# A convolution stage's end: where the modulation units run, and an output product as three rounded passes

## The chip, the cores and the metric

One core of a Trainium2 chip runs the whole program: three blocks of a network with modulated (adaptive) norms in float32, one launch. Engines are named as in the profile: PE (TensorE, matmul), PEld (its weight loads), DVE (VectorE), ACT (ScalarE), POOL (GpSimd) and SP (SyncE, which issues the DMAs). The metric is the device time of one execution in microseconds (us). The kernel before took 4165.31 us (median of 3 runs, 4162.82 to 4167.35).

## The reference, cut to what matters

The change lies in the convolution mixer of the first block. `h` is the normalized and modulated input (512 tokens of 1024 channels), and E is 2048:

```
a, g, z   = split(h @ conv_w_in + conv_b_in, 3)      # (512 x 1024) @ (1024 x 6144)
v         = a * sigmoid(g)
v         = depthwise_conv2d_rowwise(v, conv_dw, 31 taps, rows of 64) + conv_dw_b
v         = layernorm over E of v, times conv_ln_g, plus conv_ln_b
v         = silu(v) * silu(z)
x         = x + gate * (v @ conv_w_out + conv_b_out)  # (512 x 2048) @ (2048 x 1024)
```

The modulation vectors of blocks two and three are computed in the same stage, beside this, since they depend on nothing but their condition vectors:

```
mod2 = silu(c_2) @ w_ada_2 + b_ada_2                  # (1 x 1024) @ (1024 x 6144)
mod3 = silu(c_3) @ w_ada_3 + b_ada_3
```

All inputs are float32.

## The kernel before, in words

The program is a row of phases, each a block in which every engine has its own instruction list and semaphores order them; a phase begins when the one before it has ended on all engines. Activations lie transposed: channels on the 128 partitions, 512 tokens along a row. `conv_phase` (L978) is the phase in question. It runs in the trace from 1217.0 to 1821.1 us.

**Products.** 48 products in an order fixed by `by_tile` (L993): for tile i of 16, the SIG product (sigmoid gate), the A product (value), and the GATE product (outer gate) of tile i-2. Each is 8 float32 matmuls of 128x128 weights and 512 columns (L1113) into one of 6 PSUM banks used in a ring. PE's float32 matmul appears as two MATMUL records in the trace. `wait_bank` (L1029) makes PE wait until the bank's last reader is done. ACT evicts SIG (L1165) and GATE (L1168); DVE evicts A with the sigmoid into a padded grid (`padded`, L1208, instruction L1211).

**Taps.** DVE applies the 31 taps of two tiles at a time, alternating between them (L1225, L1228): 62 instructions for a pair, into `u`. PE adds up finished tiles with a matmul of ones (`total`, L1081, L1083) for the mean, five tiles behind the products.

**Modulation units.** The two 1024x6144 matrices are cut into `NA` = 48 units of 256 columns, 1 MB each, loaded by SP into two buffers `cv_ada` (`load_ada`, L1043; a load waits for the unit two before it to have been multiplied). One unit (`modulation`, L1092) is 8 matmuls of 32-column weights (L1102), in four row groups of the array's output, followed by `turn` of the unit before it (L1085, L1088, two narrow matmuls), which adds and transposes the four partial sums. ACT's `taken` (L1149) copies the unit's sums out (L1153) and then keeps the turned unit before it (`keep`, L1145, L1147). A unit's first matmul waits until ACT has copied the sums of the unit before and kept the one before that.

Where a unit runs is decided by `spread` and `unit_at` (L1003, L1004): `spread` units lie among the products, after product `FIRST + ...`, and all others follow in a loop behind the last product (L1120).

**The stage's end.** Behind the last unit PE turns it (L1123), adds the last totals (L1125), and DVE forms the mean (L1235) and subtracts it from 16 tiles (L1238). ACT adds the bias to `xT` (L1177), squares each tile (L1182, four buffers), and PE adds the squares (L1129) for the variance. ACT makes 1/sqrt with Ln and Exp (L1185, L1187). Then, tile by tile, DVE multiplies by it (L1241, L1244), ACT applies gain, bias and silu (L1190), DVE multiplies by the outer gate (L1246), and PE multiplies the tile with the 8 column blocks of `conv_w_out` into all 8 banks (L1137): 16 tiles x 8 float32 matmuls. DVE adds the banks to `xT` (L1254).

SP's queue is in program order: product weights and unit loads interleaved (L1067 to L1073), the loads of the remaining units (L1074), the last output weights (L1076).

A float32r tile holds float32 rounded to fewer mantissa bits; a matmul of two such tiles makes one pass. Other phases of this kernel already split both operands in a rounded part and a rest and add three passes: high x high, high x rest, rest x high (for example L594 to L596, L3309 to L3311).

## Time and profile before

| what | value |
|---|---|
| median of 3 runs | 4165.31 us |
| profiled execution, its own time | 4166.43 us |
| its span | 4164.7 us |
| mean granted clock of PE over the span | 0.945 |
| PE busy / DVE busy / ACT busy / POOL busy | 91% / 46% / 31% / 14% |

The span is the time from the first to the last instruction of the one profiled execution. The granted clock is 1.00 at 2.4 GHz and 0.50 at 1.2 GHz. In a row of the timeline the first number is the start of a run of like instructions, the second how long it lasts, `x16` their number, and in brackets the idle time of the engine before it and what ended it. Matmuls overlap, so a row's length is longer than the distance to the next start. In rows of groups the columns are line, engine, operation, tiles and shapes, count | busy us, mean ns of one | idle time before, and what ended it.

### The profile page before, as it was taken

Reading aid. Unit: us, or ns where it says so; the run is one execution under the profiler, and the core shown is the slowest. Engines: PE = TensorE matmul, PEld = TensorE weight load, DVE = VectorE, ACT = ScalarE, POOL = GpSimd, SP = SyncE. Lnnn points to the kernel's source line nnn. Section 1 sums busy time; section 2 is a strip of 40 time slices with the busy share of each in tenths; the row PEclk is TensorE's granted clock in tenths of the full one; section 3 lists DMA queues with packets and bytes.
Section 4 is the critical chain, followed back from the end, with each engine's and each line's share of the span. In section 5 each row is a group of like instructions: output and inputs, shape, how many; then the busy total and the mean of one; then the engine's idle time right before and its main releaser. Section 6 shows DMA issues by size and latency. Waiting matters only on the chain. (4 is left out here: it accounts for less than half of the span.)

```text
span 4164.7 us, 58511 instructions
## 1 busy us (share of the span) xinstructions
PE 3807.4 (91%) x24493; PEld 2707.3 (65%) x24493; DVE 1927.8 (46%) x3055; ACT 1290.4 (31%) x2231; POOL 580.3 (14%) x303
## 2 busy tenths in 40 slices
PE   5899999999689998989999999999898858999998
PEld 2688888888554444445455555788675847777876
DVE  1455565555419886243213323543267656245421
ACT  0544444444321121332113322432343031323321
POOL 0000000000110000010000001344361000443442
PEclk7899999999799997899889999999999979999999
DMA  8211111111235456120402113233230000432331
GB/s 298 61 42 46 52 52 37 42 52 51 61 106 168 152 156 199 49 77 27 91 8 62 45 31 101 86 97 97 62 88 18 4 1 3 114 94 84 93 92 60
DMA packets 515096, 318.67 MB, mean 77 GB/s; under 512 B 30908, under 2 KB 497397, under 8 KB 514582
## 3 DMA queue, kind: packets, MB, share of 16 engines
q1 hardware_dynamic: 514838, 314.87, 26.0%
q8 instruction: 206, 3.38, 0.3%
q14 instruction: 52, 0.43, 0.0%
HBM read 310.64 MB, written 4.19 MB: 76 GB/s over the span
## 5 line engine op out<-in xcount | busy, mean ns | idle before, releaser
L1113 PE MATMUL cv_bank<-hT,cv_w 128*128 128x512 f32 x768 | 340.2, 598 | 13.8 <-DMA cv_w<-in_conv_w_in_dram 13.8
L3274 POOL TENSOR_TENSOR tl_wl<-tl_w,tl_wh 128x1024 fp32r<-128x1024 f32 (+1 forms) x104 | 246.8, 2374 | 718.8 <-ACT tl_wh L3385 718.7
L1228 DVE SCALAR_TENSOR_TENSOR conv_u<-cv_pad,vec,conv_u 128x512 f32<-128x512 f32 x480 | 319.2, 741 | 0.0
L1113 PEld LDWEIGHTS cv_bank<-hT,cv_w 128*128 128x128 f32 x768 | 144.9, 191 | 188.2 <-issue 173.6
L2164 POOL TENSOR_TENSOR mp_wl<-mp_w,mp_wh 128x1024 fp32r<-128x1024 f32 x72 | 173.3, 2409 | 597.0 <-ACT mp_wh L2244 597.0
L3385 ACT ACTIVATE tl_wh<-tl_w 128x1024 fp32r<-128x1024 f32 (+1 forms) x104 | 108.5, 1043 | 356.8 <-PE tl_bank L3311 354.6
L594 PE MATMUL hg_bank<-hg_hh,hg_wh 128*128 128x512 f32 x512 | 208.5, 407 | 0.0
L596 PE MATMUL hg_bank<-hg_hh,hg_wl 128*128 128x512 f32 x512 | 200.3, 391 | 0.0
L595 PE MATMUL hg_bank<-hg_hl,hg_wh 128*128 128x512 f32 x512 | 199.0, 389 | 0.0
L3309 PE MATMUL tl_bank<-tl_room,tl_wh 128*128 128x512 f32 x464 | 186.8, 403 | 12.9 <-POOL tl_wl L3274 12.1
L3311 PE MATMUL tl_bank<-tl_room,tl_wl 128*128 128x512 f32 x464 | 183.2, 395 | 0.0
L3310 PE MATMUL tl_bank<-tl_room,tl_wh 128*128 128x512 f32 x464 | 181.8, 392 | 0.0
L1952 PE MATMUL at_bank<-hT,at_w 128*128 128x512 f32 x384 | 177.6, 606 | 0.0
L912 POOL TENSOR_TENSOR ho_wl<-ho_w,ho_wh 128x2048 fp32r<-128x2048 f32 x7 | 33.1, 4730 | 1015.2 <-ACT ho_wh L941 1015.2
L583 PE MATMUL hg_bank<-hg_w,hT 128*128 128x128 f32 x1024 | 133.2, 294 | 35.2 <-issue 19.3
L583 PEld LDWEIGHTS hg_bank<-hg_w,hT 128*128 128x128 f32 x1024 | 131.2, 210 | 43.5 <-issue 27.1
L2244 ACT ACTIVATE mp_wh<-mp_w 128x1024 fp32r<-128x1024 f32 x72 | 76.1, 1059 | 251.5 <-PE mp_bank L2184 244.0
L3309 PE MATMUL tl_bank<-tl_hh,tl_wh 128*128 128x512 f32 x352 | 139.4, 396 | 4.3 <-DVE tl_rest L3489 4.3
L3311 PE MATMUL tl_bank<-tl_hh,tl_wl 128*128 128x512 f32 x352 | 139.4, 396 | 0.0
L3310 PE MATMUL tl_bank<-tl_rest,tl_wh 128*128 128x512 f32 x352 | 139.3, 396 | 0.0
L2182 PE MATMUL mp_bank<-mp_dh,mp_wh 128*128 128x512 f32 x320 | 129.0, 403 | 0.0
L771 DVE TENSOR_TENSOR hg_wl<-hg_w,hg_wh 128x1024 fp32r<-128x1024 f32 x64 | 78.1, 1221 | 103.5 <-ACT hg_wh L678 103.5
(693 smaller groups left out, 8199.6 us busy)
## 6 DMA issues: line engine op xcount, KB each, us to landing
cv_ada<-in_w_ada_dram SPq DMA_DIRECT2D x48, 1024.0 KB, 7.8
hg_w<-in_hgrn_w_in_dram SPq DMA_DIRECT2D x80, 512.0 KB, 3.9
mp_w<-in_w_mlp_dram SPq DMA_DIRECT2D x64, 512.0 KB, 4.0
ada_w<-in_ada_w_dram SPq DMA_DIRECT2D x12, 2048.0 KB, 19.9
cv_w<-in_conv_w_in_dram SPq DMA_DIRECT2D x48, 512.0 KB, 4.0
tl_w<-in_w_ffn_in_dram SPq DMA_DIRECT2D x44, 512.0 KB, 3.9
fr_w<-in_w_in_dram SPq DMA_DIRECT2D x26, 512.0 KB, 3.8
at_w<-in_w_in_dram SPq DMA_DIRECT2D x24, 512.0 KB, 3.9
```

What stands on the lines that cost most here:

```text
L583: ins = pe.matmul(bank[:, t * P:(t + 1) * P], src[:, k, t * P:(t + 1) * P], W[m][:, k, :], start=(k == 0), stop=(k == KD - 1))
L594: pe.matmul(bank[:, :], wh[:, k, :], hh[:, k, :], start=(k == 0), stop=False)
L595: pe.matmul(bank[:, :], wh[:, k, :], hl[:, k, :], start=False, stop=False)
L596: ins = pe.matmul(bank[:, :], wl[:, k, :], hh[:, k, :], start=False, stop=(k == KD - 1))
L1113: ins = pe.matmul(ps[n % RING][:, :], W[n % SLOTS][:, k * P:(k + 1) * P], K.hT[:, k, :], start=(k == 0), stop=(k == KD - 1))
L1228: ins = dve.scalar_tensor_tensor(o, x, by, o, ALU.mult, ALU.add)
L1952: ins = pe.matmul(SIDE_BANK[:, :], W[n % WS][:, k, :], K.hT[:, k, :], start=(k == 0), stop=(k == KD - 1))
L2164: pool.tensor_tensor(WL[u % SPLIT][:, :, :], W[(UPS + u) % RAW][:, :, :], WH[u % SPLIT][:, :, :].bitcast(F32), ALU.subtract).then_inc(low, 1)
L3274: pool.tensor_tensor(WL[u % SPLIT][:, 0:n, :], W[u % RAW][:, 0:n, :], WH[u % SPLIT][:, 0:n, :].bitcast(F32), ALU.subtract).then_inc(low, 1)
L3309: pe.matmul(to[:, :], wh[:, wk, :], rh[:, k, :], start=first, stop=False)
L3310: pe.matmul(to[:, :], wh[:, wk, :], rl[:, k, :], start=False, stop=False)
L3311: ins = pe.matmul(to[:, :], wl[:, wk, :], rh[:, k, :], start=False, stop=last)
```

## The change

The units: `spread` becomes 38 (31 before), so 38 units lie among the products, placed by `FIRST + a * 44 // 38`. Six follow the last product. The last four (44 to 47) are put between the matmuls of the variance, behind those of tiles 4, 7, 10 and 13; ACT's `taken` of each comes after its next square, and the last turn and keep come after the variance.

The output product: `conv_w_out` and the gated tiles are split in a rounded part and a rest. ACT makes the rounded parts (`WH` of 1024 columns, `uH` of 512), DVE the rests (`WL`, `uL`), and PE makes three passes for each of the 128 matmuls. `uL` takes the place of `u` and `uH` that of `gate` in memory, `WL` that of the padded grids and `WH` that of the sigmoids. The weights' split has two buffers each; the first two are converted by ACT between the last keep and the Ln. The whole diff:

```diff
--- before.py
+++ after.py
@@ -975,7 +975,7 @@
 CW, CP, GW = 31, 15, 64
 
 
-def conv_phase(K, u, gate):
+def conv_phase(K, u, gate, uL, uH):
 
 
     nc, inp = K.nc, K.inp
@@ -999,12 +999,17 @@
     ada = [inp[name][0].rearrange("(k p) n -> p k n", p=P) for name in ("w_ada_2", "w_ada_3")]
     AC, AW = 256, 2
     NA = 2 * 6 * DM // AC
-    FIRST, OF4 = 4, 3
-    spread = OF4 * (3 * NT_ - BEHIND - FIRST) // 4
-    unit_at = {FIRST + 4 * a // OF4: a for a in range(spread)}
+    FIRST, MIXED = 4, 10
+    spread = NA - MIXED
+    unit_at = {FIRST + a * (3 * NT_ - FIRST) // spread: a for a in range(spread)}
+    beside = {4 + 3 * n: spread + 6 + n for n in range(MIXED - 6)}
     with ExitStack() as st:
         W = [K.sb(st, f"cv_w{s}", [P, KD * P]) for s in range(SLOTS)]
+        with ExitStack() as under:
+            WL = [K.sb(under, f"cv_wl{s}", [P, KD * P], F32R) for s in range(2)]
         pad = [K.sb(st, f"cv_pad{p}", [P, rows, GW + 2 * CP]) for p in range(4)]
+        with ExitStack() as under:
+            WH = [K.sb(under, f"cv_wh{s}", [P, KD * P], F32R) for s in range(2)]
         sig = K.sb(st, "cv_sig", [P, 4, T])
         mean = K.sb(st, "cv_mean", [P, T])
         rstd = K.sb(st, "cv_rstd", [P, T])
@@ -1023,6 +1028,7 @@
          bg_ok, xb_ok, out_p, out_d) = sems[SLOTS:SLOTS + 19]
         extra = K.more_sems()
         (ada_in0, ada_in1, ada_sum, ada_turn, ada_copied, ada_kept, cond_ok) = extra[:7]
+        w_high, w_low, r_high, r_low = (K.ctx.enter_context(nc.semaphore(f"conv_out_sem{n}")) for n in range(4))
         ada_in = (ada_in0, ada_in1)
         grid = lambda t: t.rearrange("q (r t) -> q r t", t=GW)
 
@@ -1117,24 +1123,29 @@
                             modulation(unit_at[n])
                     if i >= LAG:
                         total(i - LAG)
-                for a in range(spread, NA):
+                for a in range(spread, spread + 6):
                     modulation(a)
-                pe.wait_ge(ada_kept, NA - 1)
-                turn(NA - 1)
                 for i in range(NT_ + BEHIND - LAG, NT_):
                     total(i)
                 pe.wait_ge(act_free, 2 * NT_)
                 for k in range(NT_):
                     pe.wait_ge(sq_ok, k + 1)
                     pe.matmul(VAR[:, :], K.ones[:, :], sq[:, k % 4, :], start=(k == 0), stop=(k == NT_ - 1)).then_inc(var_ok, 1)
+                    if k in beside:
+                        modulation(beside[k])
+                pe.wait_ge(ada_kept, NA - 1)
+                turn(NA - 1)
                 pe.wait_ge(ln_ok, 1)
                 pe.wait_ge(ada_kept, NA)
                 for k in range(NT_):
                     n = 3 * NT_ + k
-                    pe.wait_ge(w_in[n % SLOTS], 16 * (n // SLOTS + 1))
-                    pe.wait_ge(ready, k + 1)
+                    pe.wait_ge(w_low, k + 1)
+                    pe.wait_ge(r_low, k + 1)
                     for o in range(KD):
-                        ins = pe.matmul(ps[o][:, :], W[n % SLOTS][:, o * P:(o + 1) * P], u[:, k, :], start=(k == 0), stop=(k == NT_ - 1))
+                        wh, wl = WH[k % 2][:, o * P:(o + 1) * P], WL[k % 2][:, o * P:(o + 1) * P]
+                        pe.matmul(ps[o][:, :], wh, uH[:, k, :], start=(k == 0), stop=False)
+                        pe.matmul(ps[o][:, :], wh, uL[:, k, :], start=False, stop=False)
+                        ins = pe.matmul(ps[o][:, :], wl, uH[:, k, :], start=False, stop=(k == NT_ - 1))
                         if k == NT_ - 1:
                             ins.then_inc(out_p, 1)
                     if k < NT_ - 1:
@@ -1169,9 +1180,8 @@
                                            bias=K.vec[:, a_b + 32 + j:a_b + 33 + j]).then_inc(act_free, 1)
                         if n in unit_at:
                             taken(unit_at[n])
-                for a in range(spread, NA):
+                for a in range(spread, spread + 6):
                     taken(a)
-                keep(NA - 1)
                 act.wait_ge(bg_ok, 1)
                 for o in range(KD):
                     act.activation(K.xT[:, o, :], K.xT[:, o, :], ACT.Identity, bias=bg[:, o:o + 1]).then_inc(xb_ok, 1)
@@ -1180,15 +1190,46 @@
                     if k >= 4:
                         act.wait_ge(var_ok, k - 3)
                     act.activation(sq[:, k % 4, :], u[:, k, :], ACT.Square).then_inc(sq_ok, 1)
+                    if k - 1 in beside:
+                        taken(beside[k - 1])
                 act.preload_act_table_set(LOG_EXP_SET)
+                keep(NA - 1)
+                act.wait_ge(pad_ok, NT_)
+                for k in range(2):
+                    n = 3 * NT_ + k
+                    act.wait_ge(w_in[n % SLOTS], 16 * (n // SLOTS + 1))
+                    act.activation(WH[k][:, :], W[n % SLOTS][:, :], ACT.Copy).then_inc(w_high, 1)
                 act.wait_ge(var_ok, NT_)
                 act.activation(rstd[:, :], VAR[:, :], ACT.Ln, scale=1.0 / EW, bias=K.epsc[:, 0:1]).then_inc(ln_ok, 1)
                 act.wait_ge(ln_ok, 1)
                 act.activation(rstd[:, :], rstd[:, :], ACT.Exp, scale=-0.5).then_inc(rstd_ok, 1)
-                for k in range(NT_):
+
+                def weights_high(k):
+                    n = 3 * NT_ + k
+                    act.wait_ge(w_in[n % SLOTS], 16 * (n // SLOTS + 1))
+                    if k >= 2:
+                        act.wait_ge(prod, n - 1)
+                    act.activation(WH[k % 2][:, :], W[n % SLOTS][:, :], ACT.Copy).then_inc(w_high, 1)
+
+                def activated(k):
                     act.wait_ge(scaled, k + 1)
                     act.activation(u[:, k, :], u[:, k, :], ACT.Silu, scale=K.vec[:, ln_g + k:ln_g + k + 1],
                                    bias=K.vec[:, ln_b + k:ln_b + k + 1]).then_inc(silu, 1)
+
+                def tile_high(k):
+                    act.wait_ge(ready, k + 1)
+                    act.activation(uH[:, k, :], u[:, k, :], ACT.Copy).then_inc(r_high, 1)
+
+                activated(0)
+                activated(1)
+                tile_high(0)
+                activated(2)
+                tile_high(1)
+                for k in range(2, NT_):
+                    weights_high(k)
+                    if k + 1 < NT_:
+                        activated(k + 1)
+                    tile_high(k)
 
             @block.vector
             def _(dve):
@@ -1236,14 +1277,40 @@
                 dve.wait_ge(mean_ok, 1)
                 for k in range(NT_):
                     dve.tensor_tensor(u[:, k, :], u[:, k, :], mean[:, :], ALU.subtract).then_inc(cen, 1)
-                dve.wait_ge(rstd_ok, 1)
-                for k in range(2):
+
+                def weights_low(k):
+                    n = 3 * NT_ + k
+                    dve.wait_ge(w_high, k + 1)
+                    dve.tensor_tensor(WL[k % 2][:, :], W[n % SLOTS][:, :], WH[k % 2][:, :].bitcast(F32), ALU.subtract).then_inc(w_low, 1)
+
+                def normed(k):
                     dve.tensor_tensor(u[:, k, :], u[:, k, :], rstd[:, :], ALU.mult).then_inc(scaled, 1)
-                for k in range(NT_):
-                    if k + 2 < NT_:
-                        dve.tensor_tensor(u[:, k + 2, :], u[:, k + 2, :], rstd[:, :], ALU.mult).then_inc(scaled, 1)
+
+                def gated(k):
                     dve.wait_ge(silu, k + 1)
                     dve.tensor_tensor(u[:, k, :], u[:, k, :], gate[:, k, :], ALU.mult).then_inc(ready, 1)
+
+                def tile_low(k):
+                    dve.wait_ge(r_high, k + 1)
+                    dve.tensor_tensor(uL[:, k, :], u[:, k, :], uH[:, k, :].bitcast(F32), ALU.subtract).then_inc(r_low, 1)
+
+                weights_low(0)
+                weights_low(1)
+                dve.wait_ge(rstd_ok, 1)
+                for k in range(4):
+                    normed(k)
+                gated(0)
+                gated(1)
+                tile_low(0)
+                gated(2)
+                tile_low(1)
+                for k in range(2, NT_):
+                    if k + 2 < NT_:
+                        normed(k + 2)
+                    weights_low(k)
+                    if k + 1 < NT_:
+                        gated(k + 1)
+                    tile_low(k)
                 dve.wait_ge(ada_kept, NA)
                 bias2 = K.at["ada_b2"]
                 dve.tensor_tensor(K.mod[:, 48:48 + 2 * NA, :], turned[:, :, :].rearrange("p a (j v) -> p (a j) v", v=4),
@@ -1269,9 +1336,12 @@
     K.early.close()
     norm_phase(K, [(K.xT, K.hT, T, K.at["norm_g"] + 8, 24, 32, 0)])
     with ExitStack() as st:
+        with ExitStack() as under:
+            uL = K.sb(under, "conv_low", [P, EW // P, T], F32R)
+            uH = K.sb(under, "conv_high", [P, EW // P, T], F32R)
         u = K.sb(st, "conv_u", [P, EW // P, T])
         gate = K.sb(st, "conv_gate", [P, EW // P, T])
-        conv_phase(K, u, gate)
+        conv_phase(K, u, gate, uL, uH)
 
 
 GU, GV, MQ, MV, MO, MI, MF, NQ, NKC, NKS, NVS, NKW, NVW, GA = (0, 512, 1024, 2048, 2560, 3072, 3076, 3080, 3592, 3848,
```

## Rows read from the trace of the kernel before

**Rows 1.** Busy time by stretch, all engines; columns: stretch, length, engines, PEclk, DMA share, GB/s
```profile
1616.00:1681.00 65.00, 48.13 (x347) 26.32 (x346) 17.64 (x27) 8.37 (x35) 0.00 (x0) 0.56 0.78 251
...
1688.00:1704.00 16.00, 15.67 (x32) 6.59 (x32) 8.40 (x14) 10.80 (x18) 0.00 (x0) 0.89 0.00 0
...
1708.20:1820.00 111.80, 111.76 (x256) 49.15 (x256) 22.42 (x36) 11.11 (x14) 0.00 (x0) 0.98 0.06 19
```

**Rows 2.** Timeline of DVE, the last padded tile and the mean
```profile
1592.23 0.75 DVE L1211 SCALAR_TENSOR_TENSOR cv_pad<-cv_bank,vec,cv_sig 128x512 f32<-128x512 f32 x1 [7.43 <-PE cv_bank L1113]
...
1685.96 0.69 DVE L1235 TENSOR_SCALAR cv_mean<-cv_bank 128x512 f32<-128x512 f32 x1 [52.32 <-PE cv_bank L1083]
```

**Rows 3.** Timeline of PE, two products and one unit inside the product part
```profile
1510.76 13.98 PE L1113 MATMUL cv_bank<-hT,cv_w 128*128 128x512 f32 x32
1524.67 1.07 PE L1102 MATMUL cv_bank<-cv_ada,cv_cond 128*32 128x256 f32 x16
1525.67 0.61 PE L1088 MATMUL cv_bank<-cv_pick,cv_sums 128*128 128x4 f32 x4
1526.14 1.10 PE L1083 MATMUL cv_bank<-conv_u,ones 128*128 128x512 f32 x2
```

**Rows 4.** Timeline of PE, from the last products to the output product
```profile
1616.87 1.07 PE L1102 MATMUL cv_bank<-cv_ada,cv_cond 128*32 128x256 f32 x16
...
1619.17 1.07 PE L1102 MATMUL cv_bank<-cv_ada,cv_cond 128*32 128x256 f32 x16 [0.69 <-ACT cv_turned L1147]
...
1625.20 1.93 PE L1102 MATMUL cv_bank<-cv_ada,cv_cond 128*32 128x256 f32 x16 [4.42 <-DMA cv_ada<-in_w_ada_dram]
...
1637.96 1.02 PE L1088 MATMUL cv_bank<-cv_pick,cv_sums 128*128 128x4 f32 x4
...
1681.02 4.90 PE L1083 MATMUL cv_bank<-conv_u,ones 128*128 128x512 f32 x6
1688.18 15.67 PE L1129 MATMUL cv_bank<-cv_sq,ones 128*128 128x512 f32 x32 [2.26 <-ACT cv_sq L1182]
1708.24 4.51 PE L1137 MATMUL cv_bank<-conv_u,cv_w 128*128 128x512 f32 x6 [4.39 <-DVE conv_u L1246]
```

**Rows 5.** Answer on the units' tile, 1600 to 1690 us, its 15 loads
```profile
DMA to landing us min/median/max: 5.1/5.2/8.2
```

**Rows 6.** Timeline of ACT around the variance; the square repeats, 1693.65 to 1700.52
```profile
1679.92 0.17 ACT L1147 ACTIVATE cv_turned<-cv_bank 128x8 f32<-128x8 f32 x1
...
1693.65 0.63 ACT L1182 ACTIVATE cv_sq<-conv_u 128x512 f32<-128x512 f32 x1 [0.23 <-PE cv_bank L1129]
...
1703.89 0.69 ACT L1185 ACTIVATE cv_rstd<-cv_bank,epsc 128x512 f32<-128x512 f32 x1 [1.44 <-PE cv_bank L1129]
1704.61 0.63 ACT L1187 ACTIVATE cv_rstd<-cv_rstd 128x512 f32<-128x512 f32 x1
1705.26 1.28 ACT L1190 ACT_TABLE_LOAD   x1
```

**Rows 7.** Costliest groups by shape, ACT and then DVE: conversions in other phases
```profile
L678 ACT ACTIVATE hg_wh<-hg_w 128x1024 fp32r<-128x1024 f32 x64 | 67.3, 1052 | 12.2 <-DMA hg_w<-in_hgrn_w_in_dram 7.0 <-PE hg_bank L596 5.2
...
L946 ACT ACTIVATE ho_rh<-hgrn_out 128x512 fp32r<-128x512 f32 x16 | 8.5, 615 | 1.8 <-PEq L520 1.8
...
L771 DVE TENSOR_TENSOR hg_wl<-hg_w,hg_wh 128x1024 fp32r<-128x1024 f32 x64 | 78.1, 1221 | 103.5 <-ACT hg_wh L678 103.5
L2326 DVE TENSOR_TENSOR mp_dh<-mp_relu 128x512 fp32r<-128x512 f32 x32 | 76.7, 2397 | 73.8 <-ACT mp_relu L2270 73.8
...
L964 DVE TENSOR_TENSOR ho_rl<-hgrn_out,ho_rh 128x512 fp32r<-128x512 f32 x16 | 9.8, 682 | 1.0 <-ACT ho_rh L946 1.0
```

**Rows 8.** Timeline of PE, a three-pass product beginning after 12 us of idleness
```profile
3548.27 0.79 PE L3309 MATMUL tl_bank<-tl_room,tl_wh 128*128 128x512 f32 x1 [12.07 <-POOL tl_wl L3274]
...
3552.53 0.39 PE L3310 MATMUL tl_bank<-tl_room,tl_wh 128*128 128x512 f32 x1
...
3555.28 0.39 PE L3310 MATMUL tl_bank<-tl_room,tl_wh 128*128 128x512 f32 x1
```

## The prediction, made before the changed kernel was seen

> **What bounds the kernel now.** I read four views: the busy time by stretch over the phase (1217 to 1821 us), then PE's timeline through its end, DVE's timeline over the same time, and ACT's around the variance.
>
> In the product part PE never rests. A product takes (1524.67 - 1510.76) / 2 = 6.95 us and a unit beside it 1526.14 - 1524.67 = 1.47 us [rows 3]. DVE is not the bound there: before the last padded tile it waited 7.43 us for PE [rows 2]. Behind the products stand 17 units, from 1616.87 to 1681.02, 64.2 us for 17 MB, and PE runs them at a granted clock of 0.56, near the lower level (1.2 GHz) [rows 1, 4]. The clock was high at the first two; it was low after the 4.42 us wait for the third one's data [rows 4]. A unit's matmuls then last 1.93 us instead of 1.07. DVE had ended its taps at 1685.96 - 52.32 = 1633.6 and stood 52 us [rows 2]. So the tail of units is what ends last, and after it comes a chain through all engines: totals, mean, squares with variance (15.67 us), Ln and Exp, and the output product, 111.8 us with PE as its only bound [rows 1, 4].
>
> **The change part by part**, against the profiled execution (4166.43 us, span 4164.7; the median of the runs is 1.1 us lower).
>
> *Tail of units: -42.0.* Six units stay. The sixth one's turn in the tail of before began at 1637.96 and lasted 1.02, so the totals can begin where 1638.98 is now instead of at 1681.02: 42.0 us less [rows 4]. The new tail has the same pattern: its two buffers are full at its start (the loads of units 38 and 39 are issued behind products 45 and 46, 6.95 us and more ahead, against 5.2 us to landing, 8.2 at most [rows 3, 5]), and the third unit waits as before for a load that is issued only when the first has been multiplied. If that wait were 2 us longer or gone, the term would be 40 to 46. SP's queue keeps its order: the last four output weights stay behind the unit loads, and their slots come free only with the first output tiles anyway.
>
> *Seven units more between products: +10.3.* 7 x 1.47 [rows 3]. The ends are 7 x 1.07 = 7.5, if a turn hid itself, and 7 x 3.6 = 25, if a unit cost there what it costs in the tail (1.93 + 1.02 + a gap of 0.69 us). I take 1.47, since nothing in that part changes but the density: at most seven products in a row now have a unit each, 1.5 MB in 8.4 us, that is 178 GB/s against the 251 GB/s which the tail drew [rows 1]. The last padded tile lies behind 35 units instead of 30, 7.4 us later, so the taps end near 1641. The products end at 1616.9 + 10.3 = 1627.2 and six units need until 1649.3, so the taps remain covered by 8 us. If they were late the mean would wait for them.
>
> *Four units beside the variance: +8.4.* Each adds 1.47 on PE. It also adds a stall, because ACT's next square stands in its queue behind `taken` and `keep` of the unit: they end 0.69 us after the turn (the gap in which the next unit waited for them [rows 4]), then the square takes 0.63 [rows 6]. So the square is there 1.61 + 0.69 + 0.63 = 2.9 us from the unit's start, where PE, with one square in hand, wants it at 1.47 + 0.86 = 2.3 (0.86 is the distance of the squares that PE paces, 8 of them from 1693.65 to 1700.52). That is 0.6 a unit, 2.1 with the unit. The data: a load is issued one unit ahead and 7 us of PE work before it is wanted, landing in 5.2 [rows 5]. The bounds are 4 x 1.07 = 4.3 and 4 x 3.6 = 14.4. The units 42 to 45 wait for nothing else; xT's bias (5 us on ACT) stays beside the totals and the mean, as before.
>
> *Between variance and output product: +4.5.* Before, Ln began 0.04 us after the last variance matmul and PE the output product 3.0 us after Exp's end (1705.24 to 1708.24) [rows 4, 6]. Now ACT's queue has ahead of Ln the last keep, which waits for a turn that PE issues only after the variance (0.61 + 0.17 [rows 3, 6]), and two weight conversions of 1.05 [rows 7]: 2.9 us, 2.8 more. DVE's two rests of 1.22 lie beside the second conversion, Ln and Exp. After Exp DVE normalizes four tiles (0.68 each), gates one, ACT rounds it (0.62) and DVE takes the rest (0.68): 2.7 + 0.68 + 0.62 + 0.68 = 4.7 instead of 3.0, 1.7 more [rows 7]. Ends: 2 and 8.
>
> *Output product: -21.9.* Before 111.8 us for 128 matmuls, 0.873 each. The three-pass products elsewhere give the start distance (3555.28 - 3552.53) / 12 = 0.229 us a pass [rows 8], twelve starts apart. 384 x 0.229 = 87.9. PE comes from some 8 us of rest, and at 3548.27 such a product began after 12.07 us of rest with the clock low: 4.26 us for ten passes that take 2.29 later, so 2.0 more: 89.9 [rows 8]. The other engines must keep ahead: a tile's pace is 24 x 0.229 = 5.5 us. ACT's work for a tile is 1.05 + 0.81 + 0.62 = 2.5 and DVE's 0.68 x 3 + 1.22 = 3.3 [rows 7]; silu's 0.81 is an estimate between the two ACT shapes there and does not decide. With two weight buffers, the weights of tile k are converted when tile k-2 is multiplied; then 1.05 + 1.22, the gating of the next tile and the rest of this one, 0.68 each, make 3.6, under the 5.5 that tile k-1 gives as cover. If cover were gone altogether it would cost 3.6 x 14 = 50 us. DVE's last additions (0.66 us apart) still fit between the banks' ends (0.69). Ends for the product: 88 to 111.8.
>
> The sum: -42.0 + 10.3 + 8.4 + 4.5 - 21.9 = -40.7. The profiled time becomes 4125.7 us, the median 4165.3 - 40.7 = 4124.6. No later phase changes, for a phase starts only when the last has ended everywhere.
>
> **The rivals.**
>
> *A. The clock stays low through the variance.* Each unit beside it brings a stall of 0.6 us. For it: in the tail, gaps of 0.69 us in every 3.6 went together with a low clock for 60 us [rows 1, 4]. Against: the variance of before rose to 0.89 over its stretch after a 2.26 us gap, and its dense matmuls are three times the units [rows 1, 4]. It would make 16 x 1.72 (twice 0.86) + 4 x 3.6 = 41.9 instead of 15.67 + 8.4 = 24.1: +17.8, so 4142.4. The Trainium skill (TensorE: Matmul & The Clock Gate, "A second HAM failure mode: psum-queue depth-cycling") says that short idles between groups of matmuls can make the clock swing and cost throughput; by that rule this rival would be the forecast. The trace bears it out in the tail only.
>
> *B. The output product gains nothing.* The conversions hold PE at the old 6.99 us a tile. For it: two buffers only, and four new steps a tile on two queues. Against: 3.6 us of chain under a cover of 5.5. Gain 18.8, so 4146.5.
>
> *C. Slower.* DVE's conversions beside other traffic take what the slow form of the same shape takes elsewhere, 2397 ns instead of 682 [rows 7], 3.5 times. DVE's 3.3 us a tile become 11.5, which decides from 5.5 on: 16 x 11.5 = 184 instead of 89.9, +94 on 4124.6, so 4219. Against: that slow form runs while GpSimd works, which has nothing to do in this phase (0.00 in every stretch [rows 1]); three other forms give 0.68.
>
> *D. The seven and the four units cost their tail price*, since their data come late. 11 x 3.6 = 39.6 instead of 18.7: +20.9, so 4145.5. Against: density 178 of 251 GB/s.
>
> *E. More than forecast.* The new tail's clock stays high or a wait goes: gain 47 and more, 4118 or less.
>
> **How the numbers follow.** Forecast 0.74 with a range of its own of 4119 to 4132, since its terms are open by 2 to 4 us each; A 0.07, B 0.05, D 0.05, E 0.04, C and anything else that makes it slower 0.03, and 0.02 that gains and losses cancel. The range goes to 4115 below and to 4143 above, which takes in A. A change of 0.2% is 8.3 us, about what a measurement can tell from none: faster 0.95, same 0.02, slower 0.03.
>
> **What would show it.** Right: last product near 1627; totals beginning at 1649 (before 1681); the mean there waiting for PE still, not for taps; variance stretch 24 us with a clock above 0.85; Ln 2.9 us after the last variance matmul; the output product 90 us long at 0.229 a pass without idle between tiles, starting near 1690 and the phase ending near 1780. Wrong: PE waits on `cv_wl` or `conv_low` inside the output product (B or C); a clock near 0.5 in the variance (A); PE idle on `cv_ada` among the products or the variance (D).

## The result, and the profile after

The changed kernel takes 4122.86 us (median of 4 runs, 4120.93 to 4125.83) against 4165.09 us of the kernel before (4 runs, 4162.82 to 4167.35): ratio 0.9900, 95% interval 0.9885 to 0.9916, so 42.2 us faster where 40.7 were forecast. The profiled execution took 4122.46 us, its span is 4120.8, its granted clock 0.949.

The phase begins 3.2 us earlier in this trace (first product at 1219.80 us, before at 1222.97), so parts are compared by their lengths and not by their times.

The busy time by stretch over the same parts as [rows 1]: products, tail of units, totals, variance, output product (columns as there: PE, PEld, DVE, ACT, POOL, then granted clock, DMA share, GB/s).

```profile
1223.00:1625.40 402.40, 402.40 (x1547) 179.74 (x1545) 323.04 (x492) 73.78 (x134) 0.00 (x0) 1.00 0.58 177
1625.40:1646.60 21.20, 14.59 (x121) 8.09 (x121) 13.53 (x21) 2.26 (x10) 0.00 (x0) 0.64 0.84 270
1646.60:1654.30 7.70, 5.44 (x8) 1.93 (x8) 2.20 (x4) 6.11 (x12) 0.00 (x0) 0.66 0.42 142
1654.30:1678.30 24.00, 23.33 (x115) 9.71 (x115) 8.22 (x14) 11.10 (x24) 0.00 (x0) 0.93 0.27 88
1686.70:1776.00 89.30, 89.29 (x382) 73.69 (x383) 46.09 (x62) 31.69 (x42) 0.00 (x0) 0.97 0.08 24
```

The tail shrank from 65 to 21 us and is still the part with a low clock, 0.64, while the variance with its four units has 0.93. PE is busy throughout the output product. The variance loses its clock only at its start; from 1658.62 us on, behind the low stretch, the clock is whole beside the four units:

```profile
1658.62:1678.30 19.68, 19.01 (x110) 7.93 (x108) 3.90 (x7) 8.21 (x19) 0.00 (x0) 1.00 0.33 107
```

PE's timeline, the part that answers to [rows 3]: a product and its unit start every 8.51 us where units follow every product.

```profile
1266.49 7.11 PE L1119 MATMUL cv_bank<-hT,cv_w 128*128 128x512 f32 x16
1273.54 1.07 PE L1108 MATMUL cv_bank<-cv_ada,cv_cond 128*32 128x256 f32 x16
...
1275.01 7.11 PE L1119 MATMUL cv_bank<-hT,cv_w 128*128 128x512 f32 x16
1282.05 1.07 PE L1108 MATMUL cv_bank<-cv_ada,cv_cond 128*32 128x256 f32 x16
```

And the part that answers to [rows 4]:

```profile
1625.45 1.07 PE L1108 MATMUL cv_bank<-cv_ada,cv_cond 128*32 128x256 f32 x16
...
1627.75 1.07 PE L1108 MATMUL cv_bank<-cv_ada,cv_cond 128*32 128x256 f32 x16 [0.69 <-ACT cv_turned L1158]
...
1633.08 1.94 PE L1108 MATMUL cv_bank<-cv_ada,cv_cond 128*32 128x256 f32 x16 [3.72 <-DMA cv_ada<-in_w_ada_dram]
...
1646.66 5.37 PE L1089 MATMUL cv_bank<-conv_u,ones 128*128 128x512 f32 x6
1654.29 6.23 PE L1133 MATMUL cv_bank<-cv_sq,ones 128*128 128x512 f32 x10 [2.26 <-ACT cv_sq L1192]
1660.45 1.07 PE L1108 MATMUL cv_bank<-cv_ada,cv_cond 128*32 128x256 f32 x16
...
1661.92 1.10 PE L1133 MATMUL cv_bank<-cv_sq,ones 128*128 128x512 f32 x2
1663.23 1.98 PE L1133 MATMUL cv_bank<-cv_sq,ones 128*128 128x512 f32 x4 [0.21 <-ACT cv_sq L1192]
...
1677.15 1.13 PE L1133 MATMUL cv_bank<-cv_sq,ones 128*128 128x512 f32 x2 [0.15 <-ACT cv_sq L1192]
1678.11 0.50 PE L1094 MATMUL cv_bank<-cv_pick,cv_sums 128*128 128x4 f32 x4
1686.71 0.76 PE L1146 MATMUL cv_bank<-conv_high,cv_wh 128*128 128x512 f32 x1 [8.10 <-DVE conv_low L1295]
```

To be seen: the tail of before begins again as it was, two units at the high clock, a wait for the third one's load (3.72 us, before 4.42), then 1.93 us for a unit's matmuls. The totals begin at 1646.66. Beside the variance a unit's matmuls last 1.07, its successor starts 1.47 later, and the second square after it is waited for 0.21 us. The output product starts at 1686.71 out of 8.10 us of rest.

DVE and ACT in the same stretch, answering to [rows 2, 6]:

```profile
1599.09 39.84 DVE L1269 SCALAR_TENSOR_TENSOR conv_u<-cv_pad,vec,conv_u 128x512 f32<-128x512 f32 x60
1652.07 0.69 DVE L1276 TENSOR_SCALAR cv_mean<-cv_bank 128x512 f32<-128x512 f32 x1 [13.13 <-PE cv_bank L1089]
...
1682.09 2.50 DVE L1287 TENSOR_TENSOR conv_u<-conv_u,cv_rstd 128x512 f32<-128x512 f32 x4
...
1685.88 0.69 DVE L1295 TENSOR_TENSOR conv_low<-conv_u,conv_high 128x512 fp32r<-128x512 f32 x1
```

```profile
1677.12 1.28 ACT L1195 ACT_TABLE_LOAD   x1
1678.65 0.18 ACT L1158 ACTIVATE cv_turned<-cv_bank 128x8 f32<-128x8 f32 x1 [0.25 <-PE cv_bank L1094]
1678.73 2.00 ACT L1201 ACTIVATE cv_wh<-cv_w 128x1024 fp32r<-128x1024 f32 x2
1680.63 0.67 ACT L1203 ACTIVATE cv_rstd<-cv_bank,epsc 128x512 f32<-128x512 f32 x1
1681.33 0.63 ACT L1205 ACTIVATE cv_rstd<-cv_rstd 128x512 f32<-128x512 f32 x1
1681.98 1.28 ACT L1216 ACT_TABLE_LOAD   x1
```

The taps end at 1638.9, and the mean waited 13.1 us for PE; after Exp DVE normalizes four tiles and takes the first rest at 1685.88, which is what PE waited for. On ACT the last keep and two conversions stand between the last square and Ln.

Read in this way from every run's timelines, the phase has six parts, in us: products (first product to first tail unit), tail, totals (first total behind the tail to the first variance matmul), variance (to the end of its last matmul), bridge (to the first matmul of the output product), output (to DVE's last addition). Each row is one execution, the profiled one; the changed kernel's two traces (this one and e9 below) agree within 0.2 us in every part.

| run | products | tail | totals | variance | bridge | output | phase |
|---|---|---|---|---|---|---|---|
| before | 393.9 | 64.2 | 7.2 | 15.7 | 4.4 | 112.7 | 597.9 |
| changed | 405.7 | 21.2 | 7.6 | 24.0 | 8.4 | 91.0 | 557.9 |
| forecast of the difference | +10.3 | -42.0 | 0 | +8.4 | +4.5 | -21.9 | -40.7 |
| measured difference | +11.8 | -42.9 | +0.5 | +8.3 | +4.0 | -21.7 | -40.0 |

(The "tail" of before includes the last turn, which the forecast counted there too.)

### The profile page after: what moved, and what is told of

Same layout as the page of the kernel before. It is cut to its first block and busy times, and to the rows that moved or that the text cites. A ratio compares the mean times of both kernels' runs of the same rounds, so it can differ in the third digit from the quotient of the medians.

```text
span 4120.8 us, 58846 instructions
## 1 busy us (share of the span) xinstructions
PE 3771.1 (92%) x24621; PEld 2723.2 (66%) x24621; DVE 1956.8 (47%) x3087; ACT 1312.4 (32%) x2263; POOL 580.9 (14%) x303
## 5 line engine op out<-in xcount | busy, mean ns | idle before, releaser
L3379 PE MATMUL tl_bank<-tl_room,tl_wh 128*128 128x512 f32 x464 | 188.5, 406 | 12.6 <-POOL tl_wl L3344 11.8
```

The costliest lines, as they stand in the source:

```text
L3379: pe.matmul(to[:, :], wh[:, wk, :], rh[:, k, :], start=first, stop=False)
```

## The experiments

Times are medians on the chip of the run, with the kernel before run beside them: 4165.59 for the first four, 4165.09 for the next four, 4165.14 for the last four. The first eight ran on one chip, the last four on another. Edits are shown against the changed kernel, cut to the lines that matter; `...` marks what is left out. The columns are those of the table above.

| run | median us | products | tail | totals | variance | bridge | output | phase |
|---|---|---|---|---|---|---|---|---|
| e1_units | 4146.4 | 405.4 | 21.0 | 7.6 | 24.0 | 4.8 | 112.4 | 575.2 |
| e2_passes | 4141.9 | 393.5 | 65.4 | 7.7 | 14.0 | 6.6 | 90.5 | 577.7 |
| e3_none_beside | 4133.2 | 405.6 | 39.1 | 7.2 | 15.7 | 8.4 | 89.9 | 566.0 |
| e4_wh_early | 4124.4 | 405.2 | 22.5 | 6.8 | 24.0 | 6.5 | 89.9 | 554.8 |
| e5_three_bufs | 4121.9 | 405.7 | 17.6 | 7.7 | 24.0 | 8.4 | 91.1 | 554.6 |
| e6_all_among | 4126.8 | 412.5 | 1.5 | 18.3 | 25.0 | 8.4 | 91.1 | 556.8 |
| e7_rests_on_pool | 4123.7 | 405.1 | 21.8 | 7.0 | 24.0 | 8.4 | 90.7 | 557.1 |
| e8_joined | 4118.6 | 405.7 | 17.6 | 7.8 | 22.2 | 6.2 | 89.7 | 549.3 |
| e9_changed_again | 4121.7 | 405.6 | 21.3 | 7.5 | 24.0 | 8.4 | 90.9 | 557.8 |
| e10_fill | 4123.4 | 405.1 | 23.1 | 5.3 | 24.0 | 8.4 | 90.9 | 556.8 |
| e11_joined_fill | 4113.9 | 405.6 | 16.8 | 5.3 | 22.2 | 6.2 | 89.6 | 545.7 |
| e12_joined_40 | 4109.9 | 408.2 | 9.9 | 7.3 | 20.5 | 6.2 | 90.9 | 543.0 |

(e6 has one unit behind the last product, a tail of 1.5; its totals wait for the taps. The output part varies between 89.6 and 91.1 with the number of passes at its start that still run at the low clock: fourteen in the changed kernel, seven in e11. A pass starts every 0.43 us there instead of every 0.227.)

**Each part alone.** e1 takes the output product of before with the new placement:

```diff
-                    pe.wait_ge(w_low, k + 1)
-                    pe.wait_ge(r_low, k + 1)
+                    pe.wait_ge(w_in[n % SLOTS], 16 * (n // SLOTS + 1))
+                    pe.wait_ge(ready, k + 1)
...
-                        pe.matmul(ps[o][:, :], wh, uH[:, k, :], start=(k == 0), stop=False)
-                        pe.matmul(ps[o][:, :], wh, uL[:, k, :], start=False, stop=False)
-                        ins = pe.matmul(ps[o][:, :], wl, uH[:, k, :], start=False, stop=(k == NT_ - 1))
+                        ins = pe.matmul(ps[o][:, :], W[n % SLOTS][:, o * P:(o + 1) * P], u[:, k, :], start=(k == 0), stop=(k == NT_ - 1))
```

> The placement of the units alone; the output product stays in float32 as before. Theory (the terms add, each at the size the trace of after shows for it): products longer by 11.8, tail shorter by 42.9, variance longer by 8.3, totals by 0.5, and the last turn and keep ahead of Ln 0.8, since no weights are converted: -21.5 us against before, so 4143.6. Rival 1 (the placement gives nearly all, because the three passes are paid back in the bridge and the conversions): 4125 to 4130. Rival 2 (the placement only moves the units' cost to the products, and the gain comes from the passes): 4160 or more.

e2 takes the new output product with the old placement:

```diff
-    spread = NA - MIXED
-    unit_at = {FIRST + a * (3 * NT_ - FIRST) // spread: a for a in range(spread)}
-    beside = {4 + 3 * n: spread + 6 + n for n in range(MIXED - 6)}
+    spread = OF4 * (3 * NT_ - BEHIND - FIRST) // 4
+    unit_at = {FIRST + 4 * a // OF4: a for a in range(spread)}
+    beside = {}
```

> The three-pass output product alone, with its conversions; units placed as before (31 among the products, 17 behind them, none beside the variance). Theory: the output product 21.7 shorter, 3.7 of it given back between variance and product (two weight conversions 2.0, the longer way from Exp to the first pass 1.7): -18.0 us, so 4147.1. Rival 1: -5 or less, 4160 or more. Rival 2: 40 us, 4125. With the run of the units alone it also tells whether the two parts add: theory -39.5 together; what the whole change shows above that lies outside the phase.

Measured: ratios 0.9955 (0.9942 to 0.9969) and 0.9947 (0.9934 to 0.9961), 19.2 and 23.7 us. The phase by itself gives -22.7 and -20.2, where -21.5 and -18.0 were expected. Both rivals of "one part gives nearly all" fall. The medians have the two parts in the other order than the phase has. Only the profiled execution shows its parts: e1's five runs go from 4136.7 to 4149.6, and the profiled one is the lowest, so where its other four spend 8 to 13 us more isn't known. In the phase the two parts add to -43.0, against -40.0 together. Of the 3.0, 1.4 lies in the bridge: in e2 the squares are not delayed by units, so ACT has loaded its table and begun to convert (at 1702.68 us) before the last variance matmul ends (1704.08), and the three passes lengthen the bridge by 2.2 there but by 4.0 - 0.4 = 3.6 in the joint kernel. 1.7 lies in e2's variance (14.0 against 15.7): its clock was whole from 1688.35 us on, ahead of its first matmul, while in the kernel before it was low from 1688.63 to 1692.05 us, under the variance's first matmuls. PE had waited 2.26 us ahead of it in both.

**The four units beside the variance.**

```diff
-    beside = {4 + 3 * n: spread + 6 + n for n in range(MIXED - 6)}
+    beside = {}
...
-                for a in range(spread, spread + 6):
+                for a in range(spread, NA):
                     modulation(a)
...
-                for a in range(spread, spread + 6):
+                for a in range(spread, NA):
                     taken(a)
```

> The changed kernel with none beside the variance: 38 units among the products, ten in the tail. Theory: a unit costs 3.6 us in the tail (bound by its 1 MB and by a chain of PE and ACT at the low clock) and 2.1 beside the variance, so this is 4 x 1.5 = 6 us slower than the whole change: 4129. Rival (a unit beside the variance costs as much as in the tail, since PE is the bound in both): 4123, the same as the whole change.

Measured: 4133.2, and the phase 8.1 longer than the changed kernel's. Tail +17.9 for four units, 4.5 each; variance -8.3, 2.1 each. The direction is the theory's and the rival falls. Its price of 3.6 was low: in this trace PE waited for two loads in the tail, 4.15 and 3.50 us, and not for one.

**The first two weight conversions earlier.**

```diff
+                    if k in (7, 10):
+                        m = (k - 7) // 3
+                        act.wait_ge(w_in[(3 * NT_ + m) % SLOTS], 16 * ((3 * NT_ + m) // SLOTS + 1))
+                        act.activation(WH[m][:, :], W[(3 * NT_ + m) % SLOTS][:, :], ACT.Copy).then_inc(w_high, 1)
...
-                for k in range(2):
-                    n = 3 * NT_ + k
-                    act.wait_ge(w_in[n % SLOTS], 16 * (n // SLOTS + 1))
-                    act.activation(WH[k][:, :], W[n % SLOTS][:, :], ACT.Copy).then_inc(w_high, 1)
```

> The changed kernel with the first two weight conversions on ACT between the squares of the variance (behind squares 7 and 10) instead of ahead of Ln. Theory: ACT idles 2.64 us before each later unit there, so 1.05 each is hidden, Ln comes 2.0 us earlier and so does the end: 4120.9. Rival (the conversions push squares back, PE waits for them, and what is saved ahead of Ln is spent in the variance): 4123.

Measured: the bridge is 6.5 instead of 8.4 and the variance unchanged, so the mechanism is as expected, 2.0 us, and the rival's (squares pushed back) falls. The median, 4124.4 with an interval of the ratio of 0.9886 to 0.9917, can't tell 2 us from none.

**Three buffers for the units.**

```diff
-    SLOTS, RING = 12, 6
+    SLOTS, RING = 10, 6
...
-    AC, AW = 256, 2
+    AC, AW = 256, 3
...
-        ada_in = (ada_in0, ada_in1)
+        ada_in = (ada_in0, ada_in1, extra[7])
```

> The changed kernel with three unit buffers instead of two; the memory for it is two of the twelve weight slots. Theory (the tail's six units are slow because the third waits 3.7 us for a load issued only when the first is done, and PE's clock falls in that wait): with three buffers filled at the tail's start no unit waits over 1.5 us, the clock stays high, and the load rate, 1 MB in 3.6 us behind the first, ends the tail after 14.5 us instead of 21.2: 6.5 us faster in the phase, 4116.4. Rival (the tail's pace is the units' own on PE and ACT and the clock falls anyway, or the DMA queues give the same rate from the start on): 4121 to 4123.

Measured: the tail is 17.6, so 3.6 saved where 6.7 were expected. The median, 4121.9, lies in the rival's range. PE's timeline of this run in the tail:

```profile
1632.90 1.07 PE L1108 MATMUL cv_bank<-cv_ada,cv_cond 128*32 128x256 f32 x16 [0.69 <-ACT cv_turned L1158]
...
1636.56 1.07 PE L1108 MATMUL cv_bank<-cv_ada,cv_cond 128*32 128x256 f32 x16 [2.05 <-DMA cv_ada<-in_w_ada_dram]
1637.56 0.95 PE L1094 MATMUL cv_bank<-cv_pick,cv_sums 128*128 128x4 f32 x4
1639.61 1.94 PE L1108 MATMUL cv_bank<-cv_ada,cv_cond 128*32 128x256 f32 x16 [1.10 <-DMA cv_ada<-in_w_ada_dram]
```

Three units run from their buffers, the fourth waits 2.05 us for its load and still runs at the high clock, and in the turn behind it (0.95 instead of 0.61) the clock falls. So the rival is right that it falls anyway, without a wait of over 2.05 us. A load takes longer here from issue to landing, 7.3 us (median; up to three of them at a time) against 5.2 [rows 5], but more data arrive. Here are the changed kernel's tail and this run's, busy time by stretch (last column GB/s):

```profile
1629.00:1640.00 11.00, 6.13 (x44) 3.40 (x43) 9.93 (x15) 1.27 (x6) 0.00 (x0) 0.61 0.85 273
```

```profile
1633.00:1640.00 7.00, 3.85 (x44) 2.38 (x47) 7.00 (x12) 0.90 (x4) 0.00 (x0) 0.83 1.00 327
```

The fourth and the fifth unit, which both wait for their loads, start 3.05 us apart, where the tail of two buffers goes at 3.6 us a unit. So the third buffer gives a head start of one unit and a quicker pace, until the low clock brings back the 3.6 us.

**All 44 units among the products.**

```diff
-    FIRST, MIXED = 4, 10
+    FIRST, MIXED = 4, 4
...
-    beside = {4 + 3 * n: spread + 6 + n for n in range(MIXED - 6)}
+    beside = {4 + 3 * n: spread + n for n in range(MIXED)}
...
-                for a in range(spread, spread + 6):
-                    modulation(a)
...
-                for a in range(spread, spread + 6):
-                    taken(a)
```

> The changed kernel with 44 units among the products and none in the tail; four beside the variance as in the change. Theory (the taps are the next bound: they ended at 1638.9, and every unit ahead of the last padded tile delays them by 1.6 us): products end 9.6 later, at 1635, but the taps end 5 x 1.6 = 8 later, at 1647, so the mean comes only 3 us earlier than in the change: 4120, with DVE not waiting for PE ahead of the mean. Rival (PE stays the bound): six units at 1.6 instead of 3.5 and the mean 11.6 earlier: 4111.

Measured: 4126.8, 4 us above the changed kernel where 3 us less was expected; the phase itself is 1.1 shorter. The medians' rise lies outside the phase in the profiled execution (5.6 us more there than in the changed kernel's), where the code is the same; its cause is open. PE's timeline and DVE's:

```profile
1637.47 1.96 PE L1089 MATMUL cv_bank<-conv_u,ones 128*128 128x512 f32 x4
1649.73 3.78 PE L1089 MATMUL cv_bank<-conv_u,ones 128*128 128x512 f32 x4 [10.30 <-DVE conv_u L1265]
1655.78 7.27 PE L1131 MATMUL cv_bank<-cv_sq,ones 128*128 128x512 f32 x10 [2.26 <-ACT cv_sq L1188]
```

```profile
1608.93 0.75 DVE L1248 SCALAR_TENSOR_TENSOR cv_pad<-cv_bank,vec,cv_sig 128x512 f32<-128x512 f32 x1 [10.72 <-PE cv_bank L1119]
...
1610.51 39.84 DVE L1265 SCALAR_TENSOR_TENSOR conv_u<-cv_pad,vec,conv_u 128x512 f32<-128x512 f32 x60
1653.55 0.69 DVE L1272 TENSOR_SCALAR cv_mean<-cv_bank 128x512 f32<-128x512 f32 x1 [3.21 <-PE cv_bank L1089]
```

PE now waits 10.30 us for `conv_u`: the taps end at 1650.35, 426.9 us behind the first product instead of 419.1. So the taps are the next bound, as held, and the rival (11.6 us) falls. The mean comes 430.1 us behind the first product instead of 432.3, 2.2 of the 3 us expected, and 1.0 of it is given back in the variance: the clock had fallen in PE's 10 us of rest, and the first five variance matmuls took 7.27 instead of 6.23. DVE still waits 3.21 us for PE ahead of the mean, against what was expected: that is PE's last totals, which could only begin when the taps were done.

**GpSimd beside DVE, rival C.**

```diff
+            @block.gpsimd
+            def _(pool):
+                for k in range(2, NT_):
+                    n = 3 * NT_ + k
+                    pool.wait_ge(w_high, k + 1)
+                    pool.tensor_tensor(WL[k % 2][:, :], W[n % SLOTS][:, :], WH[k % 2][:, :].bitcast(F32), ALU.subtract).then_inc(w_low, 1)
...
-                    weights_low(k)
```

> The changed kernel with the rests of the output weights, from the third tile on, made by GpSimd instead of DVE. Rival C of the prediction priced DVE's slow form, 3.5 times, and tied it to GpSimd working beside it. If that holds, DVE's 2.0 us a tile (one normalization, one gating, one rest) become 7.0, over the 5.46 us that PE takes for a tile, and the output product grows from 91 to 112: 4144. Theory (a GpSimd rest takes 2.4 us, and the chain from a free buffer to the rest, 1.05 + 2.4, stays under 5.46; DVE is slowed in part at most): the product stays at 91 us: 4123.

Measured: 4123.7, output product 90.7. Groups of this run between 1690 and 1776 us, then one tile of DVE's timeline:

```profile
L1239 POOL TENSOR_TENSOR cv_wl<-cv_w,cv_wh 128x1024 fp32r<-128x1024 f32 x14 | 33.7, 2405 | 554.7 <-ACT cv_wh L1212 554.7
L1298 DVE TENSOR_TENSOR conv_u<-conv_u,conv_gate 128x512 f32<-128x512 f32 x13 | 29.8, 2293 | 32.3 <-ACT conv_u L1216 32.3
...
L1302 DVE TENSOR_TENSOR conv_low<-conv_u,conv_high 128x512 fp32r<-128x512 f32 x15 | 12.0, 800 | 2.4 <-ACT conv_high L1221 2.4
```

```profile
1704.68 2.29 DVE L1298 TENSOR_TENSOR conv_u<-conv_u,conv_gate 128x512 f32<-128x512 f32 x1 [1.94 <-ACT conv_u L1216]
1706.89 0.68 DVE L1302 TENSOR_TENSOR conv_low<-conv_u,conv_high 128x512 fp32r<-128x512 f32 x1
1707.50 0.68 DVE L1294 TENSOR_TENSOR conv_u<-conv_u,cv_rstd 128x512 f32<-128x512 f32 x1
```

And the GpSimd instruction of the same tile:

```profile
1704.02 2.40 POOL L1239 TENSOR_TENSOR cv_wl<-cv_w,cv_wh 128x1024 fp32r<-128x1024 f32 x1 [3.04 <-ACT cv_wh L1212]
```

The slow durations are real, but they do not belong to a kind of instruction. The one DVE instruction that meets a GpSimd instruction (here the gating, 0.68 before) starts 0.66 us after it, takes 2.29 us and ends at 1706.97, 0.55 us behind the end of the GpSimd one (1706.42); the next two take 0.68 again. The price is one long instruction a tile, 1.6 us, not 3.5 times the lot; 2.29 + 0.68 + 0.68 = 3.65 stay under PE's 5.44 a tile. The Trainium skill (SBUF — State Buffer, "Terms") has DVE and GpSimd take a shared pair of ports by a lock held for the whole instruction, the loser being blocked; this trace agrees, with one blocked instruction a tile.

**Joined.** e8 has three buffers, early conversions, two squares ahead of a unit's copies, and three normalized tiles ahead of the first gating:

```diff
-    AC, AW = 256, 2
+    AC, AW = 256, 3
...
-                    if k - 1 in beside:
-                        taken(beside[k - 1])
+                    if k - 2 in beside:
+                        taken(beside[k - 2])
+                    if k in (8, 11):
+                        m = (k - 8) // 3
...
-                for k in range(4):
+                for k in range(3):
                     normed(k)
                 gated(0)
                 gated(1)
                 tile_low(0)
+                normed(3)
```

> What the trace of the changed kernel leaves: three unit buffers (-6.5), the first weight conversions beside the variance (-2.0), ACT's next two squares ahead of the copies of a unit's sums, so that PE has two in hand when a unit ends (4 x 0.45 = -1.8), and three normalized tiles instead of four ahead of the first gating (-0.4). Theory (the terms add): 4122.9 - 10.7 = 4112. Rival (each frees only what the next one then binds, above all the taps, which end at 1638.9 and leave 6 us at most): 4116 or more.

Measured: 4118.6, phase -8.6 against the changed kernel, 10.7 expected. Three buffers gave 3.6 of 6.5, the rest came as expected: variance -1.8, bridge -2.2; a further 1.3 lies in the output part, which met fewer passes at the low clock. The median is only 4.3 us below the changed kernel's and lies in the rival's range (4116 or more), but not for the rival's reason: the taps ended 9.6 us ahead of the mean. The rest of the gap between phase and median isn't explained. The clock in the tail had become the question.

**The clock in the tail.** e9 has no edit:

> The changed kernel as it is, on the same chip as the three beside it, so that differences of 2 to 5 us can be read. Expected: 4123, between 4120 and 4126.

Measured: 4121.7 (4117.8 to 4122.9). e10 adds work behind each tail unit:

```diff
+                pe.wait_ge(act_free, on_act[(SIG, NT_ - 1)] + 1)
                 for a in range(spread, spread + 6):
                     modulation(a)
+                    pe.matmul(ps[1][:, :], K.ones[:, :], K.hT[:, 0, :], start=True, stop=True)
```

> The changed kernel with one added float32 matmul of 128x128 weights and 512 columns behind each of the six tail units, into a bank that nobody reads; it is extra work and does nothing for the result. Theory (the clock is low in the tail because PE's work there is light and has gaps, not because of the one long wait; dense matmuls keep it high): the fill is hidden beside ACT's 0.69 us and the loads, the tail stays near 21 us, bound by 1 MB in 3.6 us, the totals take 2.7 us less and the variance 1.9 less: 4.6 us faster than the changed kernel. Rival (the 3.7 us wait for the third unit's load decides, and the clock stays low behind it): the fill takes 1.72 each at the low clock, 1.0 more than ACT covers, and the tail grows by 4 to 6 us.

```profile
1634.43 1.10 PE L1129 MATMUL cv_bank<-hT,ones 128*128 128x512 f32 x2
1639.08 1.91 PE L1108 MATMUL cv_bank<-cv_ada,cv_cond 128*32 128x256 f32 x16 [3.55 <-DMA cv_ada<-in_w_ada_dram]
...
1643.78 1.94 PE L1108 MATMUL cv_bank<-cv_ada,cv_cond 128*32 128x256 f32 x16
...
1647.30 1.07 PE L1108 MATMUL cv_bank<-cv_ada,cv_cond 128*32 128x256 f32 x16
...
1651.14 1.07 PE L1108 MATMUL cv_bank<-cv_ada,cv_cond 128*32 128x256 f32 x16 [1.26 <-DMA cv_ada<-in_w_ada_dram]
...
1653.55 2.74 PE L1089 MATMUL cv_bank<-conv_u,ones 128*128 128x512 f32 x6
```

Measured: 4123.4, no gain. Both theories have half of it: the clock fell at the end of the 3.55 us wait, as the rival has it, so that the third and the fourth unit took 1.91 and 1.94, and it rose again ahead of the fifth (1.07), as the theory has it; the totals took 2.74 instead of 5.37. The tail grew by 1.8, and the first variance matmuls, after a 2.56 us gap, were no faster (6.23).

e11 is e8 with the same two added lines:

> The joined version (three unit buffers, early weight conversions, squares ahead, three normalized tiles) with the same fill behind the tail units. Its waits in the tail are 2 us at most. Theory (work in the gaps keeps the clock high where no wait is over 2 us): totals 2.7 and variance 1.9 less than in the joined version, the tail 1 us less: 5 us faster than the joined version, 13 faster than the changed kernel in the phase: 4111. Rival (the light units themselves let the clock fall): the tail grows by 2 to 4 us over the joined version's 17.6.

```profile
1635.30 1.07 PE L1108 MATMUL cv_bank<-cv_ada,cv_cond 128*32 128x256 f32 x16 [0.81 <-DMA cv_ada<-in_w_ada_dram]
...
1638.29 1.07 PE L1108 MATMUL cv_bank<-cv_ada,cv_cond 128*32 128x256 f32 x16 [0.42 <-DMA cv_ada<-in_w_ada_dram]
...
1641.29 1.07 PE L1108 MATMUL cv_bank<-cv_ada,cv_cond 128*32 128x256 f32 x16 [0.42 <-DMA cv_ada<-in_w_ada_dram]
...
1643.69 2.74 PE L1089 MATMUL cv_bank<-conv_u,ones 128*128 128x512 f32 x6
```

Measured: 4113.9 (4109.5 to 4115.8), phase -3.5 against e8. With three buffers and the fill no gap is over 0.81 us, every unit takes 1.07, and the totals 2.74. The rival's price (a tail 2 to 4 us longer) falls; the tail was 0.8 us shorter than e8's. Whether it is the length of the gaps or the lightness of the work that the fill mended is not separated, for it changes both: without it, in e8, PE waited 0.69, 0.69 and 1.91 us, and the clock fell 1.2 us behind the last of these. Of the 5 expected the variance's 1.9 did not come: its clock still fell at the start. Of e11's four executions two have a mean clock of 0.952 and times up to 4112.4, two have 0.950 and times from 4115.3, so what this trace shows may not have held in every one.

e12 is e11 with 40 units among the products:

```diff
-    FIRST, MIXED = 4, 10
+    FIRST, MIXED = 4, 8
...
-    beside = {4 + 3 * n: spread + 6 + n for n in range(MIXED - 6)}
+    beside = {4 + 3 * n: spread + 4 + n for n in range(MIXED - 4)}
...
-                for a in range(spread, spread + 6):
+                for a in range(spread, spread + 4):
```

> The same as the joined version with fill, with 40 units among the products and four in the tail, of which three find their data there. Theory: products 3.3 longer, the tail 9.5 instead of 17.6, and now the taps end last, at 419.1 + 3.3 = 422.4 us behind the first product against 415.5 for PE's last unit; so the totals of the last two tiles wait for them and the mean comes about 3 us earlier than in the joined version: 3 faster than that without fill, and equal within 2 us to the joined version with fill. Rival (PE is still the bound): 6 us faster than the joined version with fill.

Measured: 4109.9 (4108.7 to 4110.4), ratio 0.9867 (0.9850 to 0.9883): the fastest kernel here, 55 us under the kernel before and 12 under the changed one. The mean waited 1.41 us for PE and PE 1.93 us for the taps, so the two meet, as the theory has it. It gains 2.7 us over e11 in the phase and 4.0 by the medians, between the theory (at most 2) and the rival (6). The variance ran wholly at the high clock (its first five matmuls in 4.53), which its forecast did not have and which gave 1.7 us. PE had waited 1.93 and 2.32 us shortly before, and the clock fell behind waits of 2.26 (the kernel before) and 2.33 us (e8) at the same place, so this part of the gain may be luck.

## Why the prediction was right

By its steps, forecast first (parts from one profiled execution each):

- *Tail, -42.0; measured -42.9.* The pattern repeated: two quick units, one wait, the rest at 3.6. The wait was 3.72 instead of 4.42.
- *Seven units among the products, +10.3; measured +11.8.* Mis-sized: 1.47 was the distance from a unit to the next product's start, but the product next to a unit takes 7.04 and not 6.86. The unit's whole price is 8.51 - 6.86 = 1.65, and 11.8 / 7 = 1.68. Rival D is out: PE was busy for all of the 402.4 us.
- *Four beside the variance, +8.4; measured +8.3*, 2.1 each, with the stall where it was put. The clock was 0.93 there, so rival A is out, and so is the rule of the Trainium skill (TensorE: Matmul & The Clock Gate, "A second HAM failure mode: psum-queue depth-cycling") for this place: idles of 0.15 to 0.21 us between groups left the granted clock at 1.00 from 1658.62 us on, and all that was lost lies at the start. e3 shows that the placement was worth 8 us.
- *Bridge, +4.5; measured +4.0.* Keep and conversions put Ln at 1680.63, 2.35 us behind the end of the last variance matmul; the forecast had 2.9. The last turn ended 0.33 us behind that matmul and not 0.61, and the two conversions took 2.00 and not 2.10. From Exp's end to PE's start 4.75, forecast 4.7.
- *Output product, -21.9; measured -21.7.* The start distance was 0.227 us a pass, fourteen slow passes at the start instead of ten. Rivals B and C needed PE to wait; it did not.
- *Not foreseen: +0.5* in the totals, whose three matmuls all ran at the low clock.
- *The taps stay covered by 8 us; measured 7.7* (1638.9 to 1646.66), and e6 and e12 confirm them as the next bound.

The errors of the parts, +1.5, -0.9, +0.5, -0.1, -0.5 and +0.2 us, cancel in part, so the sum, -40.0 against -40.7, is nearer than its terms. The medians differ by 42.2, and by 43.4 in the repeat. The span's difference of 43.9 is -3.2 ahead of the phase (first product at 1219.80 instead of 1222.97), -40.0 in it and -0.7 behind it, and the code outside is the same. Over all fourteen traces the span less the phase lies between 3559.8 and 3569.1 us; the kernel before has 3566.8 and the changed one 3562.9 and 3563.4. Whether 2 to 3 us of the gain come from there, or chance put them there, stays open.

## What to carry to other kernels

Price moved work at the place where it goes: in these traces the same unit cost 3.6 to 4.5 us behind the products (a load and a low clock), 2.1 beside the variance and 1.65 among the products. Before moving more, look for what ends next (here DVE's taps, 8 us behind), and read what stands in an engine's queue ahead of the one instruction that everybody waits for. Where the clock falls in a stretch of gaps, shorten the gaps before filling them: here the fill alone gained nothing (e10), and with a third buffer beside it the tail kept its clock in the one execution traced (e11).

## What the runs showed of the hardware that was not expected

- The granted clock fell within or at the end of PE's waits of 3.72 us (changed kernel) and 3.55 us (e10), and 1.1 to 1.2 us behind the end of waits of 2.05 us (e5) and 1.91 us (e8), which two gaps of 0.69 us had gone before. It stayed high over gaps of 0.81 us with dense work between them (e11). At the low clock a unit's matmuls took 1.93 us instead of 1.07.
- The length of a gap does not decide alone. Behind the same wait of 2.26 us ahead of the variance the clock fell in the kernel before and stayed high in e2, and in e12 it stayed high over waits of 1.93 and 2.32 us. What does decide is open.
- A DVE instruction that meets a GpSimd one ends 0.55 us behind that one's end: 2.29 us instead of 0.68 where it started 0.66 us after a GpSimd instruction of 2.40 (e7). The DVE instructions behind it take 0.68 again.
- With up to three 1 MB loads at a time each lands in 7.3 us where fewer took 5.2, but the rate rises: 327 GB/s in e5's tail against 273 in the changed kernel's, where PE itself took 3.6 us for a unit of 1 MB and so may have set the pace.
